# Two fixed experts, a 96-row beside a 32-row expert, a spread order of positions, and reordered loads in a one-core block kernel

## The reference

```python
mod = c @ w_ada + b_ada                      # 6 x 1024 values
sh1, sc1, g1, sh2, sc2, g2 = split(mod, 6)
h = modulate(rms_norm(x, norm_mix_g), sh1, sc1)
proj = h @ w_in                              # 1024 -> 3080
...                                          # short convolution (y_a) and scan (y_b)
x = x + g1 * (concat(y_a, y_b) @ w_out)
h = modulate(rms_norm(x, norm_ffn_g), sh2, sc2)
scores = sigmoid(h @ w_router)               # the 8 experts of each token
out = (silu(h @ ws_gate) * (h @ ws_up)) @ ws_down
for e in range(64):
    out += gates[:, e] * ((silu(h @ we_gate[e]) * (h @ we_up[e])) @ we_down[e])
return rms_norm(x + g2 * out, norm_final_g)
```

## Time and profile before

| | |
|---|---|
| median of 3 runs | 707.0 us (706.34 to 707.13) |
| profiled execution | 704.53 us |
| its span, first to last instruction | 702.8 us |
| PE busy | 643.3 us, 92% |
| DVE, ACT, POOL busy | 37%, 18%, 6% |
| moved by DMA | 250.97 MB, mean 357 GB/s |
| mean granted clock of PE | 0.976 |

### The profile page before, as it was taken

How to read it: one execution, slowest core, us unless ns; L and a number is a source line. 1 busy time by engine, 2 the same in 40 slices (tenths; PEclk the granted TensorE clock), 3 DMA queues, 4 the chain that set the end, 5 groups by cost and what they waited for, 6 DMA issues and landing times.

```text
span 702.8 us, 11377 instructions
## 1 busy us (share of the span) xinstructions
PE 643.3 (92%) x4248; PEld 369.5 (53%) x4248; DVE 261.7 (37%) x717; ACT 126.5 (18%) x279; POOL 43.2 (6%) x223
## 2 busy tenths in 40 slices
PE   2599999769998899999999999999999999997982
PEld 0288878524544554556555565455554545553540
DVE  0167848684373233132332313323233232331125
ACT  1321221201310111111111111111111111110112
POOL 7000000000201000000000000000000000000000
PEclk9899999979999999999999999999999999998997
DMA  8998891942039999999999999999999999999961
GB/s 309 376 405 334 336 410 57 370 193 118 0 127 424 422 418 421 421 422 419 420 421 420 422 420 421 421 421 420 421 422 419 422 419 421 420 419 422 420 253 61
DMA packets 40026, 250.97 MB, mean 357 GB/s; under 512 B 4705, under 2 KB 6817, under 8 KB 11937
## 3 DMA queue, kind: packets, MB, share of 16 engines
q1 hardware_dynamic: 38256, 248.56, 86.2%
q10 hardware_dynamic: 1714, 1.67, 0.7%
HBM read 249.17 MB, written 1.05 MB: 356 GB/s over the span
## 4 chain that ended last, share of the span: by engine, by line
PE 75%; DMA 13%; DVE 8%; issue 1%; ACT 1%; ACTq 1%; SPq 0%; DVEq 0%
PE PS L1538 10%; PE PS L1534 9%; PE PS L1517 8%; PE PS L1544 8%; PE PS L1331 8%; DMA ring<-in_we_up_dram 7%; PE PS L1592 5%; PE PS L1570 5%; PE PS L1566 5%; DMA ring<-in_w_ada_dram 5%; PE PS L1575 4%; PE PS L1447 3%; PE PS L1588 2%; DVE MOD L856 2%; PE PS L1553 2%; DMA ring<-in_w_out_dram 1%
## 5 line engine op out<-in xcount | busy, mean ns | idle before, releaser
L1538 PE MATMUL PS<-ring,arena 128*64 128x256 f32 x736 | 88.4, 391 | 0.3 <-DMA ring<-in_we_up_dram 0.3
L1331 PE MATMUL PS<-hT,ring 128*128 128x256 f32 x384 | 84.7, 380 | 0.0
L1156 DVE SCALAR_TENSOR_TENSOR arena<-arena,gate,PS 128x128 f32<-128x128 f32 (+1 forms) x48 | 17.9, 373 | 175.8 <-ACT arena L782 175.8
L1331 PEld LDWEIGHTS PS<-hT,ring 128*128 128x128 f32 x384 | 72.5, 190 | 11.0 <-issue 1.5
L1167 DVE TENSOR_TENSOR YLO<-PS,YHI 128x512 fp32r<-128x512 f32 x57 | 39.3, 689 | 93.3 <-ACT YHI L793 93.3
L1517 PE MATMUL PS<-G,H2HI 128*128 128x256 f32 (+1 forms) x256 | 69.6, 307 | 1.3 <-ACT arena L773 0.7
L1544 PE MATMUL PS<-ring,arena 128*32 128x256 f32 x1024 | 63.9, 401 | 6.4 <-DMA ring<-in_we_up_dram 6.4
L1534 PE MATMUL PS<-ring,arena 128*128 128x512 f32 x144 | 66.4, 612 | 0.6 <-issue 0.6
L1538 PEld LDWEIGHTS PS<-ring,arena 128*64 128x64 f32 x736 | 49.9, 134 | 31.7 <-issue 2.6
L793 ACT CAST YHI<-PS 128x512 fp32r<-128x512 f32 x57 | 33.4, 585 | 169.4 <-PE PS L1570 79.7
L1517 PE MATMUL PS<-G,H2LO 128*128 128x256 f32 (+1 forms) x256 | 62.1, 278 | 0.0
(11 more groups left out here) (257 smaller groups left out, 596.4 us busy)
## 6 DMA issues: line engine op xcount, KB each, us to landing
ring<-in_we_gate_dram SPq DMA_DIRECT2D x64, 1024.0 KB, 18.1
ring<-in_we_up_dram SPq DMA_DIRECT2D x64, 1024.0 KB, 20.7
ring<-in_we_down_dram SPq DMA_DIRECT2D x64, 1024.0 KB, 19.1
ring<-in_w_ada_dram SPq DMA_DIRECT2D x6, 3072.0 KB, 14.8
ring<-in_w_in_dram SPq DMA_DIRECT2D x3, 3072.0 KB, 16.2
ring<-in_w_ada_dram SPq DMA_DIRECT2D x3, 2048.0 KB, 7.5
ring<-in_w_out_dram SPq DMA_DIRECT2D x1, 3072.0 KB, 19.1
ring<-in_w_in_dram SPq DMA_DIRECT2D x1, 1568.0 KB, 27.8
```

Of the source, the lines that this page charges most:

```text
L1331: mm = pe.matmul(PS[:, 2 + q % QB, 0:TOK], w[:, k, (m % 6) * P:(m % 6) * P + P], hT[:, k, :], start=(k == 0), stop=(k == KD - 1))
L1538: m = pe.matmul(PS[64 * c:64 * c + 64, 6, 0:FE].rearrange("p (a n) -> p a n", a=2), xt[:, k, :], gu_cols(w[0], k, c), start=(k == 0), stop ...
```

## The change

It does these things:

- Two experts are fixed instead of one. Expert 0 goes to slot 2 and expert 1 to slot 0, both ahead of the sort.
- A fourth kind of position, mixed, holds one expert with up to 96 rows and one with up to 32. Its gate and up is computed in four groups of 32 rows, three from the one expert and one from the other. There are 9 mixed positions, 1 wide, 23 narrow and 11 pairs in 15 units, where there were 9 wide, 23 narrow and 16 pairs in 16 units. The ranks are: 1 expert with 128 rows, 7 with 96, 23 with 64, the others 32; the two fixed ones have 96.
- The second part of `w_out` goes to slot 1 ahead of `ada(7)`'s part, and the shared expert to slot 3 (freed by the last input projection) behind it.
- The bias of the first modulation parts comes as 16 rows of a small table and is added to `AB1` in three small DVE steps instead of two; four broadcast loads of 64 KB are gone. The loads for `hrow`, `dskip`, `rbias` and `MOD` stand behind the work on x, and SP's next load no longer waits for them.
- PE's first transpose waits for `ident` alone, and two ACT functions of one element (Sqrt) load its table early, at the start and before the last position's end.
- The sort has six small DVE steps for the capacity where it had four.

```diff
-FIXED = 1
-WIDE, NARROW, PAIR = "wide", "narrow", "pair"
-UNITS = ([[WIDE, PAIR, NARROW]]
-         + 4 * [[PAIR, NARROW, WIDE], [NARROW, PAIR, WIDE], [NARROW, PAIR, NARROW]]
-         + 3 * [[NARROW, PAIR, NARROW]])
+FIXED = 2
+WIDE, MIXED, NARROW, PAIR = "wide", "mixed", "narrow", "pair"
+UNITS = [[PAIR, NARROW, MIXED],
+         [NARROW, PAIR, NARROW],
+         [MIXED, NARROW, PAIR],
+         [NARROW, MIXED, NARROW],
+         [MIXED, NARROW, PAIR],
+         [MIXED, NARROW, PAIR],
+         [WIDE, PAIR, NARROW],
+         [PAIR, NARROW, NARROW],
+         [MIXED, NARROW],
+         [MIXED, NARROW, PAIR],
+         [NARROW, MIXED, NARROW],
+         [NARROW, NARROW, PAIR],
+         [NARROW, NARROW, NARROW],
+         [MIXED, NARROW, PAIR],
+         [NARROW, PAIR, NARROW]]
...
-N_EXP = {WIDE: 1, NARROW: 1, PAIR: 2}
-ROWS = {WIDE: 128, NARROW: 64, PAIR: 32}
+ROWS = {WIDE: [128], MIXED: [96, 32], NARROW: [64], PAIR: [32, 32]}
 EXPERTS = []
-for p, kind in enumerate(KIND):
-    if p < 2 * FIXED and kind == WIDE:
-        EXPERTS.append([p // 2])
-    else:
-        first = max([FIXED - 1] + [q for qs in EXPERTS for q in qs]) + 1
-        EXPERTS.append(list(range(first, first + N_EXP[kind])))
+fixed, ranked = list(range(FIXED)), list(range(FIXED, NE))
+for kind in KIND:
+    first = [fixed.pop(0)] if fixed and kind == MIXED else []
+    EXPERTS.append(first + [ranked.pop(0) for _ in ROWS[kind][len(first):]])
...
-SLOT, USE = [2, 0, 3, 4, 1], [1] * NSLOT
+SLOT, USE = [2, 0, 1, 4, 3], [1] * NSLOT
...
-         (I, 0, 3), (A, 6, 2), (O, 0, 0), (A, 7, 2), (S, 0, 1), (A, 8, 2), (O, 1, 3)]
+         (I, 0, 3), (A, 6, 2), (O, 0, 0), (O, 1, 1), (A, 7, 2), (S, 0, 3), (A, 8, 2)]
...
-            act.dma_start(prm[R_NM:R_END, :], norm_mix_g[0].rearrange("(b q) -> b q", q=P)).then_inc(params_in, 16)
-            act.dma_start(hrow[:, 0, :], ssm_dt_bias[0].partition_broadcast(P)).then_inc(small_in, 16)
-            act.dma_start(hrow[:, 1, :], ssm_a_log[0].partition_broadcast(P)).then_inc(small_in, 16)
-            for half in range(2):
-                act.dma_start(dskip[HD * half:HD * half + HD, :],
-                              ssm_d[0].rearrange("(b q) -> q b", q=2)[half].partition_broadcast(HD),
-                              allow_slow_non_contiguous=True).then_inc(small_in, 16)
-            act.dma_start(rbias[:], router_bias[0].partition_broadcast(P)).then_inc(small_in, 16)
+            act.dma_start(prm[R_NM:R_BA, :], norm_mix_g[0].rearrange("(b q) -> b q", q=P)).then_inc(params_in, 16)
+            act.dma_start(prm[R_BA:R_END, :], b_ada[0, 0:2 * D].rearrange("(b q) -> b q", q=P)).then_inc(params_in, 16)
             act.nop().then_inc(small_issued, 1)
-            for g in range(4):
-                act.dma_start(bias1[32 * g:32 * g + 32, :],
-                              b_ada[0, 512 * g:512 * g + 512].partition_broadcast(32)).then_inc(bias1_in, 16)
-            act.wait_ge(mod_zero, 1)
-            act.dma_start(MOD[0:1, 2 * D:6 * D], b_ada[0:1, 2 * D:6 * D]).then_inc(bada_in, 16)
-
-
+            act.wait_ge(ident_ready, 1)
+            act.activation(small[:, 15:16], ident[:, 0:1], ACT.Sqrt)
...
+            act.dma_start(hrow[:, 0, :], ssm_dt_bias[0].partition_broadcast(P)).then_inc(hrow_in, 16)
+            act.dma_start(hrow[:, 1, :], ssm_a_log[0].partition_broadcast(P)).then_inc(hrow_in, 16)
...
+            act.dma_start(rbias[:], router_bias[0].partition_broadcast(P)).then_inc(small_in, 16)
...
-            dve.wait_ge(small_in, 16 * 5)
-            dve.wait_ge(bias1_in, 16 * 4)
             dve.wait_ge(ada_used, 3)
-            dve.tensor_tensor(mod1, bank(1), bias1, ALU.add).then_inc(mod1_ready, 1)
+            dve.tensor_copy(mod1, bank(1)).then_inc(mod1_ready, 1)
...
+            link(dve.tensor_tensor(AB1[:, 0:KD], PS[:, 0, KD:2 * KD], COL[:, R_BA + KD:R_END], ALU.add))
+            link(dve.scalar_tensor_tensor(out=AB1[:, 0:KD], in0=AB1[:, 0:KD], scalar=1.0, in1=COL[:, R_NM:R_BA],
+                                          op0=ALU.add, op1=ALU.mult))
+            link(dve.tensor_tensor(AB1[:, KD:2 * KD], PS[:, 0, 0:KD], COL[:, R_BA:R_BA + KD], ALU.add), ab1_ready)
...
-                link(dve.tensor_scalar(more, rank, NWIDE - 0.5, 64.0, ALU.is_lt, ALU.mult))
-                link(dve.tensor_tensor(cap, more, capcol[0:NE, :], ALU.add))
-                link(dve.tensor_scalar(more, rank, NWIDE + NNARROW - 0.5, 32.0, ALU.is_lt, ALU.mult))
-                link(dve.tensor_tensor(cap, cap, more, ALU.add))
+                for n, rows in enumerate((96, 64, 32)):
+                    link(dve.tensor_scalar(more, rank, N_OVER[rows] - 0.5, 32.0, ALU.is_lt, ALU.mult))
+                    link(dve.tensor_tensor(cap, more, cap if n else capcol[0:NE, :], ALU.add))
...
-            pe.wait_ge(consts, 1)
-            pe.wait_ge(params_in, 16 * 5)
+            pe.wait_ge(ident_ready, 1)
+            pe.wait_ge(params_in, 16 * 6)
...
+                    elif KIND[p] == MIXED:
+                        for r0, r1, u in ((0, 32, 0), (32, 64, 0), (64, 96, 0), (96, 128, 1)):
+                            m = pe.matmul(PS[r0:r1, 6, :].rearrange("p (a c n) -> p a c n", a=2, c=FT),
+                                          xt[:, k, r0:r1], gu_cols(w[u], k), start=(k == 0), stop=(k == KD - 1))
...
+                    elif KIND[p] == MIXED:
+                        for r0, r1, u in ((0, 32, 0), (32, 64, 0), (64, 96, 0), (96, 128, 1)):
+                            m = pe.matmul(PS[r0:r1, 5, :], HTT[:, p % 2, cc * P + r0:cc * P + r1],
+                                          w[u][:, cc, 512 * half:512 * half + 512], start=(cc == 0),
+                                          stop=(cc == FT - 1))
```

More of the change, by code:

```diff
@@ L75 @@
     USE.append(USE[PROC[q - NSLOT]] + 1)
-NWIDE = KIND.count(WIDE) - FIXED
-NNARROW = KIND.count(NARROW)
-KIND_OF = [KIND[p] for p in POS_OF]
-RANK = [{WIDE: 0, NARROW: NWIDE, PAIR: NWIDE + NNARROW}[KIND_OF[q]] + KIND_OF[FIXED:q].count(KIND_OF[q])
-        for q in range(FIXED, NE)]
+ROWS_OF = [ROWS[KIND[p]][EXPERTS[p].index(q)] for q, p in enumerate(POS_OF)]
+N_ROWS = {rows: ROWS_OF[FIXED:].count(rows) for rows in (128, 96, 64, 32)}
+N_OVER = {rows: sum(n for more, n in N_ROWS.items() if more > rows) for rows in N_ROWS}
+RANK = [N_OVER[ROWS_OF[q]] + ROWS_OF[FIXED:q].count(ROWS_OF[q]) for q in range(FIXED, NE)]
+MAXE = max(len([q for p in range(NPOS) if UNIT_OF[p] == i for q in EXPERTS[p]]) for i in range(len(UNITS)))
 NCOL = 4
@@ L800, in _ @@
                     silu_gate(p + 1)
+                else:
+                    act.activation(small[:, 15:16], ident[:, 0:1], ACT.Sqrt)
                 for pairs in gather_steps(p):
@@ L1648, in _ @@
                 gather(i + 1, early)
-                if p and not (KIND[p] == WIDE and KIND[p - 1] != WIDE):
+                if p and not halves(p) > halves(p - 1):
                     add_up(p - 1)
@@ L1652, in _ @@
                 down(p, 0)
-                if p and KIND[p] == WIDE and KIND[p - 1] != WIDE:
+                if p and halves(p) > halves(p - 1):
                     add_up(p - 1)
```

57 lines of the change are left out of this document (35 added, 22 removed).

## The result

The changed kernel takes 699.37 us in the median of four executions (698.76 to 700.12); the kernel before, measured beside it, 706.67 (706.09 to 707.13). The ratio is 0.9905, with a 95% interval of 0.9886 to 0.9924. The profiled execution took 698.76 us, its span is 697.0 us: 5.8 us less than the 702.8 of before. Predicted were 700.5 us and a span of 696.35. In the runs further down two single executions took 1634 us (the kernel before) and 2965 us (three fixed experts); without them the medians there move by 0.1 us at most.

A forecast was written before the change was run, and what follows sets the result against it. The prediction took the expert stage to be bound by DMA's weight stream. Its terms, -7.5 - 1.6 + 0 + 0.35 + 2.3 = -6.45 us on a span of 702.8, gave a span of 696.35 and a median of 700.5 us, range 696 to 704.

The forecast's parts named there:

- DMA never pauses and PE does; the stage is bound by the stream: Expert stage: DMA's weight stream is the bound; one expert load less behind the sort gives -7.5 us.
- the stream's start: First expert loads behind the sort: queue stays covered, taken as 0, with up to 2.3 us of pause.
- First loads, -1.6: Kernel's start: small loads removed or moved behind let PE begin projections earlier, -1.6 us, between -0.3 and -3.1.
- all of the loss: The -3.1 us bound of the first loads term: all the DMA time lost at the start comes back.
- Output projection, 0 (-1.7 to +1.0): Early second part of `w_out` gains at most 1.7 us; PE's wait for `ada(8)` and slow clock cost 1.75 to 2.75.
- Sort, +0.35: Sort ahead of the stream: two more steps at 0.14 to 0.18 us each, +0.35 us.
- Mixed gate and up, 7.4 us: Mixed positions: 64 instructions of 512 columns by 32 rows on PE take 4 x 1.85 = 7.4 us.
- The end, +2.3: Last pair: PE waits 5 to 6 us, clock falls, gate and up slows by 2.6; 2.3 us reach the end.
- 0 if the wait stays near 3 us: Lower bound of the end term: no cost if PE's wait before the last pair stays near 3 us.
- The clock falls in more than one place: Rival 3, expert stage: PE falls to 1.2 GHz at many positions, +3 us on the forecast, 703.5; chance 0.07.
- Rival 4: Mixed positions: gate and up of about 10 us uses up PE's 28 us of slack; at 12, 719 us; chance 0.07.

The follow-up runs named there:

- old order: Changed kernel with the order and slots of the output and shared weights' loads as before: 697.93 us.
- small loads first: Changed kernel with the small broadcast loads (`hrow`, `dskip`, `rbias`) issued again ahead of x and the large weights: 701.27 us.
- late rows: Changed kernel with the two late mod rows of the output projection moved one quarter later: 694.03 us.
- both kinds of filler: Two runs, each the changed kernel with added matmuls, results unused: in the wait before the last pair's gate and up, 698.15 us; between the first ada parts, 702.3 us.
- the last run: Changed kernel with mod rows one quarter later and 20 added matmuls ahead of the last pair's gate and up: 692.1 us, ratio to before 0.979.
- the experiment: For the first loads, the run small loads first (701.27 us); for the output projection, the run old order (697.93 us).

## Why the prediction was right, and where it was not

The time (700.5 for 699.37) and the side were right, and so was the main term. Other terms were off and made up for each other.

- **"DMA never pauses and PE does; the stage is bound by the stream": right.** One expert less gave 6.35 us in the median. The forecast's 7.49 was the interval of a load; over seven traces with two fixed experts in the mixed order and no added stalls (changed, old order, small loads first, late rows, both kinds of filler, and the last run) the stretch from first sorted issue to last pair is 458.7 us in the mean, 6.7 less than before. Of the 0.8 us that remain changed's trace shows 0.6 at the stream's start, where it runs at 397 GB/s in 216 to 220 and at 406 in 230 to 240; I had put that at 0, with up to 2.3.
- **First loads, -1.6: of the right size.** The trace shows -2.40, the experiment 1.9. The landing moved for certain: PE's wait for the second `w_ada` part ends at 21.7 to 22.1 us in all ten traces with these first loads, 1.6 to 2.1 ahead of before. What PE makes of it differs: in the same ten the 24 instructions behind that wait took 4.1 to 5.35 us, by where the clock fell, and ada part 7 was issued at 117.45 to 119.96. Changed's trace is the earliest of them, so its -2.40 is partly luck. (The bound of -3.1, "all of the loss", is more than its 1.4, its 0.8 and a few tenths come to.) The trace of before also was an execution 2 us under its median. That the small loads cause the loss is borne out by the stretch of 8 to 12 us; that they do it by holding up the queue isn't shown, since the large load behind them was also issued 2.4 us later before than it is now, which I had not counted.
- **Output projection, 0 (-1.7 to +1.0): the mechanism right, the size outside its bounds.** That PE would wait for `ada(8)` until 153.9 less the shift, and that the clock would fall, came as written. The mod rows began at 151.55 instead of 155.46, 1.5 us beyond the shift of 2.4, near the bound of 1.7. But the slow clock cost 1.9 us in them and 1.3 in the quarters behind, 3.2 where I had 2.75 at most and 1.75 at least; 0.4 came back from a wait for DVE that went. That is +1.3 in the trace, 1.4 in the experiment. I had the wait in hand and asked only what it costs, not what PE could do meanwhile. That was worth 5.3 us.
- **Sort, +0.35: right** (+0.36).
- **Mixed gate and up, 7.4 us: right** (7.39 to 7.46 where the clock stood, 10.08 once).
- **The end, +2.3: mis-sized, 1.2.** I computed a wait of 5 to 6 us before the last pair, and named one of 4 to 6 us as a sign; it was 2.67. PE's work between was as I had it: from 620.25 to 659.6 it takes 39.3 us. But I let it begin with the landing of expert 56. The mixed gate and up began only 42.0 us ahead of the last pair's, where six loads at 7.49 take 44.9, and without a wait: by this estimate PE was 2.9 us behind. It had lost 2.6 of them at 472.99, where the gate and up took 10.08 instead of 7.46 us, and nothing gave them back before the last pair. In the last run, where the clock held at that place, PE takes 183.9 us from there to the last pair without its waits and the added matmuls, in changed 186.6. So with a full clock at 472.99 the wait would have been about 5.3 us. And the bound "0 if the wait stays near 3 us" was wrong: the clock fell behind 2.67 us. It cost 1.6 us of work, 1.2 at the end. The 2.3 that I took is what two other traces show, those whose gate and up took 6.6 us; which of the two comes is a matter of when the clock falls and rises.
- **The clock falls in more than one place: right as far as it went.** Of changed's seven waits for weights three have a fall behind them: at 224.71 (a wait of 2.84 us, then 5.44 for a narrow gate and up), 472.99 (3.82) and 662.26 (2.67). At the first two the stream bounds and nothing was lost in time by it; the second only shortened a later wait. The chance of 0.07 for it as a cost was fair. By the rule of the Trainium skill ("TensorE: Matmul & The Clock Gate", section on HAM oscillation) bursts shorter than their waits fall back each time. The trace of before agrees at its start: 4.76 us of work, a wait of 6.10, and then 4.45 us for 24 instructions that take 2.78 at the full clock. But the falls of the expert stage aren't of this kind: PE works for 439.3 of 464.8 us there, longer between two waits than it waits, and the clock falls behind some of them all the same. That holds for 639.5 in the trace of before too, which I had put down to this rule.
- **Rival 4, "PE has 28 us of slack, used up when gate and up takes about 10 us": the length held** (10.3 us cost 11.6 us), the number behind it did not. The 28 was the stream's time less PE's busy time; of the 25.5 us of the changed trace only 13.4 are waits for weights, and only these are room. At 10 us the loss isn't about to begin, as I said, but already past 11; it begins at about 8.9.

The medians don't close fully. With one fixed expert, the new first loads (-1.9), the new order (+1.4), the sort (+0.4) and the slow clock at the end (+1.2) should give +1.1 against before; measured is -0.5. The mixed positions may be worth something there too, or it is the scatter of four differences of medians. This is left open.

## What to carry to other kernels

In a stage bound by a stream, a transfer moved into an empty queue ahead of it is worth one interval, as long as it doesn't take the buffers with which the stream must open: the second one paid, the third, in the one order of positions that was run, cost more than it saved. The room of the engine that isn't the bound is nearer to the sum of its waits for the stream (13.4 us here) than to the span less its busy time (25.5). And where a wait only moves when its load comes earlier, look for independent work that stands behind it in program order: moving two rows by one quarter brought 5.3 us, where the whole change brought 7.3.
